# One layer of a diffusion step: residual rows and expert sums kept as two half-width arrays

## The reference

```
x = x + g1 * einsum(o, w_out)                       # x1
h2 = rmsnorm(x, norm2_g) * (1 + sc2) + sh2
gate, idx = lax.top_k(swapaxes(softmax(h2 @ w_router), 1, 2), cap)   # cap = 64 of 512, 16 of 128
xs = h2[idx]                                        # 16 experts x 80 rows x 2048
hid = silu(xs @ w_gate) * (xs @ w_up)               # 2048 -> 1024
out = (hid @ w_down) * gate                         # 1024 -> 2048
x = x + g2 * zeros(n, d).at[idx].add(out)
y = rmsnorm(x, final_norm_g)
```

## Time and profile before

| | |
|---|---|
| median of three runs | 2202.74 us |
| profiled execution, its own time | 2204.5 us |
| its span | 2202.7 us |
| TensorE busy | 2096.1 us, 95% of the span |
| VectorE, ScalarE, GpSimd busy | 39%, 24%, 8% |
| moved by DMA | 623.82 MB, mean 283 GB/s |
| TensorE's mean granted clock | 0.981 of full speed |

### The profile page before, as it was taken

One profiled execution on the slowest core, in us unless ns is written; L12 is line 12 of the kernel. 1 busy time (PEld: TensorE's weight loads), 2 busy tenths in 40 slices (PEclk: granted clock), 3 DMA queues, 4 the chain that ended last, 5 costly groups with the idle time before them and its releaser, 6 DMA issues.

```text
span 2202.7 us, 35849 instructions
## 1 busy us (share of the span) xinstructions
PE 2096.1 (95%) x15268; PEld 1158.4 (53%) x15268; DVE 859.0 (39%) x1306; ACT 533.7 (24%) x907; POOL 170.8 (8%) x233
## 2 busy tenths in 40 slices
PE   5899999999999999999949999999999999999994
PEld 2568888778878787888713333333333333333331
DVE  3249879225558877776231111111111111110114
ACT  4432222212257774221211001111101111110103
POOL 1020100000000001111120000000000000000001
PEclk8999999999999999999979999999999999999997
DMA  9966666552220007655679999999999999999997
GB/s 370 387 204 211 206 232 232 208 208 77 69 87 1 1 1 276 212 164 195 249 221 398 405 399 396 411 393 400 407 400 397 397 396 411 397 408 395 412 397 298
DMA packets 129308, 623.82 MB, mean 283 GB/s; under 512 B 13040, under 2 KB 14584, under 8 KB 68400
## 3 DMA queue, kind: packets, MB, share of 16 engines
q1 hardware_dynamic: 104736, 514.38, 58.8%
q0 software_dynamic: 18000, 94.74, 14.0%
q10 hardware_dynamic: 6496, 13.67, 1.8%
HBM read 593.18 MB, written 29.58 MB: 283 GB/s over the span
## 4 chain that ended last, share of the span: by engine, by line
PE 87%; DMA 4%; SPq 3%; DVE 3%; issue 1%; ACT 1%; POOL 0%; DVEq 0%; ACTq 0%; POOLq 0%
PE ps L1159 28%; PE ps L1166 14%; PE ps L652 10%; PE ps L654 10%; PE ps L653 10%; PE ps L965 3%; PE ps L1003 3%; SPq L736 2%; PE ps L979 1%; DMA arena<-acc_d 1%; DMA arena<-in_w_expert_up 1%; DMA arena<-in_w_in 1%; PE ps L889 1%; PE ps L1146 1%; PE ps L931 1%
## 5 line engine op out<-in xcount | busy, mean ns | idle before, releaser
L1159 PE MATMUL ps<-arena 128*32 128x512 f32 x6144 | 702.5, 594 | 1.6 <-DMA arena<-in_w_expert_up 0.6
L1159 PEld LDWEIGHTS ps<-arena 128*32 128x32 f32 x6144 | 197.4, 110 | 445.3 <-issue 428.3
L1166 PE MATMUL ps<-arena 128*32 128x512 f32 x3072 | 373.4, 593 | 2.8 <-DMA arena<-in_w_expert_down 2.2
L652 PE MATMUL ps<-B_w_hi,B_x_hi 128*128 128x512 f32 x720 | 287.1, 399 | 1.8 <-DVE B_x_lo L1905 1.0
L654 PE MATMUL ps<-B_w_lo,B_x_hi 128*128 128x512 f32 x720 | 281.4, 391 | 0.0
L653 PE MATMUL ps<-B_w_hi,B_x_lo 128*128 128x512 f32 x720 | 281.3, 391 | 0.0
L1166 PEld LDWEIGHTS ps<-arena 128*32 128x32 f32 x3072 | 99.4, 110 | 228.2 <-issue 224.3
L1901 DVE TENSOR_TENSOR B_w_lo<-arena,B_w_hi 128x1024 fp32r<-128x1024 f32 x72 | 87.5, 1220 | 188.2 <-ACT B_w_hi L1321 188.0
L652 PEld LDWEIGHTS ps<-B_w_hi,B_x_hi 128*128 128x128 f32 x720 | 135.5, 188 | 43.4 <-issue 11.5
L2145 DVE TENSOR_TENSOR arena<-ps,A 128x384 f32<-128x384 f32 (+1 forms) x102 | 31.0, 372 | 307.8 <-PE ps L1146 298.9
L654 PEld LDWEIGHTS ps<-B_w_lo,B_x_hi 128*128 128x128 f32 x720 | 135.6, 188 | 29.2
(11 more groups left out here) (254 smaller groups left out, 2014.2 us busy)
## 6 DMA issues: line engine op xcount, KB each, us to landing
arena<-in_w_expert_gate SPq DMA_DIRECT2D x128, 1024.0 KB, 15.0
arena<-in_w_expert_up SPq DMA_DIRECT2D x128, 1024.0 KB, 13.8
arena<-in_w_expert_down SPq DMA_DIRECT2D x128, 1024.0 KB, 15.7
arena<-in_w_mod POOLq DMA_DIRECT2D x48, 1024.0 KB, 5.3
arena<-in_w_in SPq DMA_DIRECT2D x36, 1024.0 KB, 5.3
arena<-in_w_mod SPq DMA_DIRECT2D x64, 512.0 KB, 11.6
arena<-in_w_out SPq DMA_DIRECT2D x16, 1024.0 KB, 7.0
arena<-in_w_mod POOLq DMA_DIRECT2D x64, 256.0 KB, 3.4
```

Of the source, the lines that this page charges most:

```text
L652: eng.matmul(out, x_hi, w_hi, start=start, stop=False)
L1159: mm = pe.matmul(bank(b)[32 * q:32 * q + 32, :], rows[:, 32 * (q % 2):32 * (q % 2) + 32], w_pair[q // 2], start=start, stop=stop, skip_gro ...
L1166: mm = pe.matmul(bank(b)[32 * q:32 * q + 32, :], rows, w_four[q], start=start, stop=stop, skip_group_check=True)
```

## The change

Both arrays are cut into a left and a right array of 1024 columns, so that a row has 4 KB in each. Each expert's gather becomes three indirect DMAs (left, right, factors) in place of two; each adding scatter becomes two, and its left one is issued when the left half of `xrow_out` is scaled. Each sums_back becomes two DMAs of 512 KB, and the final gather two. The quarter stores go to the array that holds their columns, in the same number and sizes. The counts of the waits follow.

```
-        acc_d = nc.dram_tensor("acc_d", [TOK, D], F32, kind="Internal").ap()
-        x1_d = nc.dram_tensor("x1_d", [TOK, D], F32, kind="Internal").ap()
+        acc_h = [nc.dram_tensor(f"acc_d{h}", [TOK, D // 2], F32, kind="Internal").ap() for h in range(2)]
+        left_right = (slice(0, D // 2), slice(D // 2, D))
+        x1_h = [nc.dram_tensor(f"x1_d{h}", [TOK, D // 2], F32, kind="Internal").ap() for h in range(2)]
...
-                sp.dma_start(finals[t], acc_d[P * t:P * (t + 1), :]).then_inc(x_in[t], 16)
+                for h in range(2):
+                    sp.dma_start(finals[t][:, left_right[h]], acc_h[h][P * t:P * (t + 1), :]).then_inc(x_in[t], 16)
...
-                for dst in (x1_d, acc_d):
-                    act.dma_start(dst[:, cols].rearrange("(t p) n -> p t n", p=P), x1[:, :, cols]).then_inc(early_stored, 16)
+                for dst in (x1_h[n // 2], acc_h[n // 2]):
+                    act.dma_start(dst[:, part].rearrange("(t p) n -> p t n", p=P), x1[:, :, cols]).then_inc(early_stored, 16)
...
-                for cols, rows in ((slice(0, D), x1_d), (slice(D, D + ROW_PAD), rstd_d)):
+                for cols, rows in ((left_right[0], x1_h[0]), (left_right[1], x1_h[1]), (slice(D, D + ROW_PAD), rstd_d)):
                     pool.indirect_dma_start(xs[0:CAP, cols], None, rows[:, :],
...
             for e in AHEAD:
-                for dst, rows in ((ahead[e - 1], x1_d), (rstdP[:, e - 1, :], rstd_d)):
+                for dst, rows in ((ahead[e - 1][:, left_right[0]], x1_h[0]), (ahead[e - 1][:, left_right[1]], x1_h[1]),
+                                  (rstdP[:, e - 1, :], rstd_d)):
...
-                pool.wait_ge(rows_ready, e + 1)
-                pool.indirect_dma_start(acc_d[:, :], bass.IndirectOffsetOnAxis(ap=idxC[:, e:e + 1], axis=0),
-                                        xrow_out[0:CAP, :], None, compute_op=ALU.add).then_inc(scattered, 16)
-                pool.wait_ge(scattered, 16 * (e + 1))
+                for h in range(2):
+                    pool.wait_ge(rows_ready, 2 * e + h + 1)
+                    pool.indirect_dma_start(acc_h[h][:, :], bass.IndirectOffsetOnAxis(ap=idxC[:, e:e + 1], axis=0),
+                                            xrow_out[0:CAP, left_right[h]], None, compute_op=ALU.add).then_inc(scattered, 16)
+                pool.wait_ge(scattered, 32 * (e + 1))
...
-            pool.indirect_dma_start(xs[0:CAP, 0:D], None, acc_d[:, :],
-                                    bass.IndirectOffsetOnAxis(ap=idxC[:, NE - 1:NE], axis=0)).then_inc(gathered, 16)
+            for h in range(2):
+                pool.indirect_dma_start(xs[0:CAP, left_right[h]], None, acc_h[h][:, :],
+                                        bass.IndirectOffsetOnAxis(ap=idxC[:, NE - 1:NE], axis=0)).then_inc(gathered, 16)
...
-                    ins = dve.scalar_tensor_tensor(out=xrow_out[0:CAP, cs], in0=xrow_out[0:CAP, cs], scalar=gcol[:, 0:1],
-                                                   in1=G2[0:CAP, cs], op0=ALU.mult, op1=ALU.mult)
-                ins.then_inc(rows_ready, 1)
+                    dve.scalar_tensor_tensor(out=xrow_out[0:CAP, cs], in0=xrow_out[0:CAP, cs], scalar=gcol[:, 0:1],
+                                             in1=G2[0:CAP, cs], op0=ALU.mult, op1=ALU.mult).then_inc(rows_ready, 1)
```

More of the change, by code:

```diff
@@ L804, in sums_back @@
             def sums_back(t):
-                sp.dma_start(finals[t], acc_d[P * t:P * (t + 1), :]).then_inc(x_in[t], 16)
+                for h in range(2):
+                    sp.dma_start(finals[t][:, left_right[h]], acc_h[h][P * t:P * (t + 1), :]).then_inc(x_in[t], 16)
             for j in range(XCH):
                 if j == XCH - 3:
-                    sp.wait_ge(scattered, 16 * (NE - 1))
+                    sp.wait_ge(scattered, 32 * (NE - 1))
                 if j >= XCH - 3:
@@ L1463, in store_rows @@
             def store_rows(n):
-                cols = slice(NB * n, NB * (n + 1))
-                for dst in (x1_d, acc_d):
-                    act.dma_start(dst[:, cols].rearrange("(t p) n -> p t n", p=P), x1[:, :, cols]).then_inc(early_stored, 16)
+                cols, part = slice(NB * n, NB * (n + 1)), slice(NB * (n % 2), NB * (n % 2 + 1))
+                for dst in (x1_h[n // 2], acc_h[n // 2]):
+                    act.dma_start(dst[:, part].rearrange("(t p) n -> p t n", p=P), x1[:, :, cols]).then_inc(early_stored, 16)
             for i in range(HI_D, 32 + HI_D - 2):
@@ L1495, in scale_gathered @@
                 if n in AHEAD:
-                    act.wait_ge(rows_ahead, 32 * len(AHEAD))
+                    act.wait_ge(rows_ahead, 48 * len(AHEAD))
                     rows, factor = ahead[n - 1], rstdP[0:CAP, n - 1, 0:1]
                 else:
-                    act.wait_ge(gathered, 32 * (n + 1 - (len(AHEAD) if n > 0 else 0)))
+                    act.wait_ge(gathered, 48 * (n + 1 - (len(AHEAD) if n > 0 else 0)))
                     rows, factor = xs, xs[0:CAP, D:D + 1]
@@ L1509, in final_squares @@
             def final_squares(t):
-                act.wait_ge(x_in[t], 48)
+                act.wait_ge(x_in[t], 64)
                 if t > 0:
@@ L1529, in _ @@
                 if e > 0:
-                    act.wait_ge(scattered, 16 * e)
+                    act.wait_ge(scattered, 32 * e)
                 if e == NE - 1:
@@ L1543, in _ @@
             for h in range(2):
-                act.wait_ge(rows_ready, NE + h)
+                act.wait_ge(rows_ready, 2 * (NE - 1) + h + 1)
                 act.wait_ge(f_squared, NT + h)
@@ L1652, in _ @@
                 pool.wait_ge(x1_done, NT * 3 + t + 1)
-                for dst, stored in ((x1_d, raw_stored), (acc_d, acc_stored)):
-                    pool.dma_start(dst[P * t:P * (t + 1), cols], x1[:, t, cols]).then_inc(stored, 16)
+                for dst, stored in ((x1_h[1], raw_stored), (acc_h[1], acc_stored)):
+                    pool.dma_start(dst[P * t:P * (t + 1), NB:], x1[:, t, cols]).then_inc(stored, 16)
             pool.wait_ge(ms2_ready, 1)
@@ L1699, in _ @@
             pool.tensor_tensor(rrow, ssr[:, 0:1], mhalf[0:CAP, 0:1], ALU.pow).then_inc(frstd_ready, 1)
-            pool.wait_ge(rows_ready, NE + 2)
+            pool.wait_ge(rows_ready, 2 * (NE - 1) + 3)
             pool.wait_ge(y_out, 16 * NT)
@@ L1705, in _ @@
                                     xrow_out[CL:CAP, :], None).then_inc(scattered, 16)
-            pool.wait_ge(scattered, 16 * (NE + 1))
+            pool.wait_ge(scattered, 32 * NE)
         @block.vector
@@ L2225, in _ @@
             dve.wait_ge(con_taken, NE + 1)
-            dve.wait_ge(gathered, 32 * (NE - len(AHEAD)) + 16)
+            dve.wait_ge(gathered, 48 * (NE - len(AHEAD)) + 32)
             for h, taken, at_least in ((0, half_taken, NE), (1, y_taken, NE + 1)):
```

## The result

The changed kernel takes 2211.3 us (median of 7 runs, 2206.4 to 2212.17) against 2202.74 us (2201.46 to 2206.58, 7 runs beside them). The medians differ by 8.6 us. The ratio, taken over all runs, is 1.0032, with a 95% interval from 1.0023 to 1.0041, and that is 7 us: beyond the 4.4 us that can be told from no change, and inside the range of 2197.5 to 2213.0. So the time lies in the range, but the likeliest case, a loss of 2.4 us, is not what happened. A second set of runs on another chip says the same (ratio 1.0029 [1.0018, 1.0040]). The profiled execution took 2208.68 us, with a span of 2206.9.

A forecast was written before the change was run, and what follows sets the result against it. It took TensorE as the bound to about 1436 us, then the DMA engines with a backlog. First gather 0.3, gathers ahead 0, DMA work 1.2 and sums_back 0.9 gave +2.4 us on 2202.74: 2205.1 us, range 2197.5 to 2213.0.

The forecast's parts named there:

- likeliest case: Whole kernel: 0.3 + 0 + 1.2 + 0.9 = +2.4 us, 2205.1 us; chance 0.51, own range 2202 to 2207.
- row rival: From 1438 us, part of the transfers' surplus goes with rows, above all in adding scatters: 2210.6 us; chance 0.29.
- What bounds the kernel: TensorE sets the pace to about 1436 us, then the DMA engines; from 1438 us each microsecond of DMA work counts.
- First gather: Start, TensorE idle until expert 0's rows land: the factors' later third issue costs +0.3 us, bounds 0 and 1.2.
- Gathers ahead: Experts 1 to 5, during expert 0: last issue 7.3 us later, at 1142.3, rows still ready in time; cost nothing.
- Scatter's issue and waits: GpSimd issuing two scatter halves: landing at most a microsecond or two later, 12 us of cover; cost nothing.
- DMA work from 1438 us: Ten gathers at 0, eleven scatters at +0.11 us each for more, smaller packets: +1.2 us.
- mixing rival: Half rows mixed with weight packets free DMA engines of a third of the 1.75 us per transfer: 2197.3 us; chance 0.2.
- Sums_back: At the end, 40 more packets an engine by 0.022 us: +0.9 us where TensorE already waits; bounds 0 and 0.9.

The follow-up runs named there:

- early gathers: Kernel before (whole rows) with the gathers of experts 7 to 15 issued four experts earlier; 2203.87 us, ratio 0.9996.
- the measurement: Kernel before with gathers, adding scatters and direct loads added behind its end, nothing beside them; run once, 2320.37 us with the added work.
- after again: The changed kernel once more, unaltered, on another chip beside the kernel before; 2210.42 us, ratio 1.0029.
- the sums alone: Only the sums lie in two arrays, x1 in one as in the kernel before; 2203.43 us, ratio 1.0000.
- own semaphore: Changed kernel, but expert 1's gathers have a semaphore of their own, apart from experts 2 to 5; 2204.01 us, ratio 1.0002.
- weights held: Changed kernel, but SP issues no weight piece of expert 0's second half until the gathers of experts 1 to 5 land; 2203.04 us, ratio 0.9997.
- spread kernel: Kernel before, gathers of experts 7 to 15 issued in the turns of experts 1, 2, 4, 5, 7, 8, 10, 11, 13; ratios 0.9979, 0.9985.
- halved version: Changed kernel with a separate semaphore for expert 1's gathers and later gathers spread over experts 1 to 13; 2213.11 and 2214.36 us, ratios 1.0034 and 1.0042.

## Why the prediction came out as it did

The range held, and that was luck: the time lies in the part that was kept of the row rival, and the row rival is out. The likeliest case, +2.4 us in 2205.1, did not come. Step by step:

- **What bounds the kernel: right, with one limit.** Spreading the gathers removed the waits and 3 to 5 us. But "each microsecond of DMA work added comes out at the end" holds only when the lag has reached the slots' 26 us; the early gathers show that where the work lies counts as much as its sum. And the backlog differs from run to run: the same code reached 23.3 us at expert 13 in the measurement, with no wait there.
- **First gather, +0.3: the size is small, the sign was wrong.** From first issue to ScalarE it takes 6.00 us instead of 6.24, below the bound of 0, and so in every profile: 5.74 to 6.12 with halves, 6.10 to 6.48 with whole rows. The later third issue is hidden, as argued. Why the halves are sooner stays open.
- **Gathers ahead, "Cost nothing": this is the step that failed.** The issue time was right (1142.81 for 1142.3) and the reader came at 1155.27, not at 1149 to 1151. Two assumptions broke. I wrote that "the DMA engines' work bounds it, not the issue": 80 rows of 4 KB take 80 x 0.268 / 16 = 1.34 us of each engine and an issue 1.2, but each expert has a third issue that carries next to nothing, so 3.6 us of issue stand against about 2.7 of data. With whole rows it was 2.4 against 2.95 (80 x 0.589 / 16). The bound changed sides. And the gathers ran on into the weights, where equal turns with packets half as large cost another 6.7 us. The cover was 3.3 us too short; the reduced clock behind the wait added 1.7. The prediction named this very wait as what would make it wrong, but gave it no chance.
- **Scatter's issue and waits, nothing: right.** The left issue takes 2.06 to 2.28 us and the right one 1.39 to 1.43 (before, 1.39 to 1.49 for the whole), but the last scatter is in by 2123.17, before SP needs it at 2134.8.
- **DMA work from 1438 us, +1.2: mis-sized, it is about 0.** The scatter's packets are exactly half as long, the gather's less than half (16.1% of 13 us and 16 engines over 160 rows is 0.209, for 0.455), the landing at expert 13 is 25.4 us as before, and the experts' period is the same. So the row rival is out, although its 2210.6 is nearest to the time: the right number for the wrong reason. The mixing rival is out too: the weights' packets beside the gather stay at 0.347 us (0.349 before), and the wait at 2010 is there. The first wait stayed in expert 13, where I had it one expert earlier.
- **Sums_back, +0.9: too small in the profile, and for another reason.** E grew by 2.0 us: 0.35 are waits for weights, and 1.6 the lower clock behind the second wait, a term that the sum doesn't have. All five profiles with halved sums and late weights at the end have a wait more (0.28 to 0.47 us, then 2.24 to 2.27), and none with whole sums has; three of the five have the lower clock behind it (after, after again, the sums alone), own semaphore and weights held don't. E also moves by itself: 58.43 and 57.06 in two kernels with whole sums. With the lag at 18.7 us the halves add nothing there. They cost only where weights are late already.

That the kernel before lost 3.1 us in a stretch that the changed one doesn't have was in its trace, in view of anyone who reads TensorE at 1138, and I had passed over it. Against a run without that stretch the change costs more.

## What to carry to other kernels

Halving a transfer's rows left its engine time alone here but not its place in the line: it doubles the issues, and beside a queue of larger packets each turn carries half the bytes. Ask of each cut transfer which of issue and data is the longer one now, and who waits for the last of them on one shared semaphore. A ring of buffers hides a lag up to its own length, here about 26 us for 12 pieces; spread the extra transfers so that the lag never gets there, rather than move them all to where there seems to be room.

## What the runs showed of the hardware

- Queues share the engines by packets, not by bytes, and small packets count: 225 packets of q0 (158 of them rows of 4 KB) against 232 of q1 in 8 us, 0.65 MB against 1.77.
- A direct load on 80 partitions takes an engine 0.594 us per 8 KB and one on 128 takes 0.319; gathered by indices on 80 it is 0.589.
- An adding scatter alone is not quite by bytes: in windows of one transfer, 0.757 us per row of 8 KB and 0.433 per 4 KB. Beside weights it is (0.658 and 0.329).
- An issue of an adding scatter takes GpSimd 1.39 to 1.49 us, also after 44 us of idle time. The left half's, which begins while the vector engine still scales the right half, takes 2.06 to 2.28.
- TensorE can slow to one matmul per 0.6 to 2.1 us while gathers move on the DMA engines, in 5 of 14 profiles: for 3 us before and 2 to 3 us in the spread kernel, for 13 in its halved version. The cause is open.
